# A buffer of zeros moved onto a table's place, with a wait for its transfer

## What is computed

```python
ada = c_act @ w_ada[l] + b_ada[l]
sh_m, sc_m, g_m, sh_f, sc_f, g_f = jnp.split(ada, 6, axis=-1)
h = modulate(rms_norm(x), sh_m, sc_m)          # h*(1+scale)+shift
proj = h @ w_in[l]
z, u = proj[..., :D_SHIFT], proj[..., D_SHIFT:]
...
# s5_mix(u, ...): 32 groups, 16 channels and 64 states each
abar_re = mag * jnp.cos(dt * a_im)             # and abar_im
bbar_re = coef_re[..., None] * b_re - coef_im[..., None] * b_im
bu_re = jnp.einsum("gpc,btgc->tbgp", bbar_re, ug)
_, _, s_re, s_im = lax.associative_scan(_ssm_combine, (a_seq_re, a_seq_im, bu_re, bu_im), axis=0)
y = einsum("gcp,tbgp->btgc", c_re, s_re) - einsum("gcp,tbgp->btgc", c_im, s_im) + d_skip * ug
```

## Time and profile before

| what | us |
|---|---|
| time, median of 3 runs | 1687.66 |
| lowest and highest of them | 1687.02, 1688.44 |
| the profiled execution's own time | 1687.02 |
| its span | 1685.2 |

### The profile page before, as it was taken

One profiled execution on the slowest core, in us unless ns is written; L12 is line 12 of the kernel. 1 busy time (PEld: TensorE's weight loads), 2 busy tenths in 40 slices (PEclk: granted clock), 3 DMA queues, 4 the chain that ended last, 5 costly groups with the idle time before them and its releaser, 6 DMA issues.

```text
span 1685.2 us, 23778 instructions
## 1 busy us (share of the span) xinstructions
PE 1507.8 (89%) x10024; PEld 1173.4 (70%) x10024; DVE 812.8 (48%) x1291; ACT 581.0 (34%) x1002; POOL 267.4 (16%) x224
## 2 busy tenths in 40 slices
PE   6979877877889999999989899998898999998989
PEld 3657666865668888888866687766686667766767
DVE  7783439623653233223354554546534455445552
ACT  4355231125333222222223434224522444232441
POOL 0000323000101011100012223222201233222220
PEclk9999987988999999999979999998998999999999
DMA  9212572162122222233221121111122111111121
GB/s 367 69 59 61 94 140 104 52 226 88 63 75 88 100 94 94 95 125 100 89 88 40 48 76 63 62 39 50 52 99 96 36 63 59 67 65 36 50 88 63
DMA packets 51849, 144.17 MB, mean 86 GB/s; under 512 B 13216, under 2 KB 17952, under 8 KB 50976
## 3 DMA queue, kind: packets, MB, share of 16 engines
q1 hardware_dynamic: 51744, 142.65, 26.4%
HBM read 137.95 MB, written 4.69 MB: 85 GB/s over the span
## 4 chain that ended last, share of the span: by engine, by line
PE 69%; DVE 14%; ACT 9%; issue 4%; POOL 2%; DMA 1%; SPq 0%; DVEq 0%; ACTq 0%
PE b L391 68%; ACT arena L2103 5%; DVE arena L1245 4%; DVE ring L1245 2%; DVE arena L1253 2%; ACT ring L2106 1%; PE b L394 1%; ACT L2103 1%; POOL arena L2734 1%; DVE arena L1933 1%; DVE X L1245 1%; ACT arena L2106 1%; DVE arena L2066 1%; DMA arena<-scr_yd 1%; DVE arena L1891 1%
## 5 line engine op out<-in xcount | busy, mean ns | idle before, releaser
L391 PE MATMUL b<-tile,ring 128*128 128x512 f32 x2288 | 702.9, 402 | 19.8 <-DVE ring L1245 9.2
L391 PE MATMUL b<-HR,ring 128*128 128x512 f32 (+1 forms) x1888 | 626.2, 408 | 63.1 <-DVE ring L1245 35.1
L391 PEld LDWEIGHTS b<-tile,ring 128*128 128x128 f32 x2288 | 437.5, 192 | 127.6 <-issue 19.5
L391 PEld LDWEIGHTS b<-HR,ring 128*128 128x128 f32 (+1 forms) x1888 | 363.6, 193 | 165.2 <-issue 61.0
L1245 DVE TENSOR_TENSOR ring<-ring,ring 128x1024 fp32r<-128x1024 f32 x186 | 256.1, 1379 | 299.9 <-ACT ring L2106 299.0
L391 PE MATMUL b<-arena 64*64 64x64 f32 (+10 forms) x3072 | 237.5, 289 | 42.9 <-issue 24.6
L2106 ACT ACTIVATE ring<-ring 128x1024 fp32r<-128x1024 f32 x186 | 195.7, 1054 | 213.9 <-PE b L391 213.4
L391 PEld LDWEIGHTS b<-arena 64*64 64x64 f32 (+5 forms) x3072 | 153.6, 150 | 115.8 <-issue 80.7
L2106 ACT ACTIVATE arena<-b 128x512 f32<-128x512 f32 (+3 forms) x136 | 74.4, 570 | 254.3 <-PE b L391 206.3
L1245 DVE TENSOR_TENSOR arena<-arena 128x512 f32<-128x512 f32 (+7 forms) x194 | 100.3, 549 | 71.2 <-ACT arena L2103 50.2
L2731 POOL TENSOR_TENSOR tile<-arena,tile 128x512 fp32r<-128x512 f32 x38 | 51.0, 1348 | 462.2 <-ACT tile L2106 462.2
(11 more groups left out here) (112 smaller groups left out, 1018.8 us busy)
## 6 DMA issues: line engine op xcount, KB each, us to landing
ring<-in_ws SPq DMA_DIRECT2D x218, 512.0 KB, 3.5
arena<-in_ws SPq DMA_DIRECT2D x15, 512.0 KB, 15.4
arena<-in_lw SPq DMA_DIRECT2D x2, 1280.0 KB, 5.6
X<-in_xT SPq DMA_DIRECT2D x2, 1024.0 KB, 6.2
arena<-scr_kpad SPq DMA_DIRECT2D x8, 256.0 KB, 12.5
X<-in_xT SPq DMA_DIRECT2D x1, 2048.0 KB, 15.3
outT<-X SPq DMA_DIRECT2D x8, 256.0 KB, 2.0
arena<-in_cst SPq DMA_DIRECT2D x1, 1088.0 KB, 5.0
```

The costliest lines, as they stand in the source:

```text
L391: return self.e.matmul(out, lhsT, rhs, start=start, stop=stop, skip_group_check=True)
```

## The change

The source of the zeros becomes a full 16 x (32 x 112) buffer over the first 14 KB of `VT`, where it was 16 x 112 at a place of its own, read 32 times over by a step of zero. Since `VT` is now written over what the transfer reads, VectorE waits for the transfer's landing before the first write of `VT`.

```diff
@@ Plan.views
-        self.TT, self.VM, self.zero = R(110, 32, 128), R(110, 16, 2, 128), R(131.75, 112)[0:16]
+        self.TT, self.VM, self.zero = R(110, 32, 128), R(110, 16, 2, 128), R(110, 32, 112)[0:16]
@@ Vector.s5_tables
             V(BB[:, ri], BB[:, ri], t, op)
         yield
+        self.wait_ge(k.s("kpad", 16), "zero")
         for dst, n, p0, p1, a, b, op in (
                 (VT[:, :, 0], 8, PR, PI, BB[:, 0], BB[:, 1], ALU.subtract),
@@ Sync.program
         self.wait_ge(k.s("mat_pool"), "zero")
-        self.e.dma_start(d["kpad"].rearrange("g c n -> c g n")[:, :, 0:112],
-                         k.zero.unsqueeze(1).broadcast_to((16, 32, 112))).then_inc(*k.s("kpad", 16).inc("zero"))
+        self.e.dma_start(d["kpad"].rearrange("g c n -> c g n")[:, :, 0:112], k.zero).then_inc(*k.s("kpad", 16).inc("zero"))
```

## The result

The changed kernel took 1712.67 us, the median of 4 runs (1705.23 to 1714.95), beside 1688.05 us for the kernel before in the same comparison (4 runs, 1687.02 to 1697.04). The ratio is 1.0127, with a 95% interval of 1.0081 to 1.0173. On 1688.05 that is 21.4 us, interval 13.7 to 29.2. The prediction was 1708.0, in a range of 1705.5 to 1711.5, slower. By the ratio the time is 1688.05 x 1.0127 = 1709.5; the median as it stands lies 1.2 us over the range's upper end.

A forecast was written before the change was run, and what follows sets the result against it. The start was taken as bound by a chain through ScalarE and VectorE, not TensorE. Stall 21.1 less slack 0.97 gave 20.2, plus 0.3 for the clock: 20.5 us over the 1687.66 median, said as 1708, range 1705.5 to 1711.5.

The forecast's parts named there:

- The landing: Zeros' transfer, last in SyncE's full queue: lands at 39.3 us, 16.1 after issue, as before; floor 38.6, the last unit's landing.
- The early landing: Rival: the 16.1 us are this transfer's own slowness and vanish; landing at 27.8, +8.7 us, 1696.4 us; chance 0.03.
- The stall and the slack: VectorE before the first VT operation: 21.1 us of stall less 0.97 of slack, a shift of 20.2 us.
- The memset: GpSimd's zeroing at the kernel's start: 32 times the columns, about 3.0 us, hidden, cost nothing.
- The late rival: Rival: late landing or late memset, zeros landing at 43.2 or 44.2, +24 to +25 us, 1712 or 1713; chance 0.07.
- The issue: SyncE issuing the zeros: 2.98 us before, perhaps 0.43 without the step of zero; saving hidden, 0.
- Who waits behind it: After VectorE's stall: TensorE, SyncE's later loads and ScalarE resume 20.2 us later; at most about 0.5 us comes back.
- The other side: Rival, not slower: a later stretch paced by the weight stream takes the stall back, 1688 us; chance 0.03.
- The clock after the rest: TensorE's lower-clock stretch after its longer idle time, at the projection's start: costs 0 to 0.6 us more, 0.3 taken.
- Each stretch as long as before: Sign for the changed profile: stretches to the end unchanged; wrong if first projection matmul to end differs by over 1 us.
- with about 1 us of scatter: Allowance for scatter and reshuffling later in the kernel, widening the forecast's 1707.2 to 1709.3 to 1706 to 1710 us.
- The upper bound of 21.6 us: Upper end of the forecast slowdown, whose lower end, 19.5 us, was the landing's floor; this forecast had chance 0.87.

The follow-up runs named there:

- the runs behind 12 to 18 units: Changed kernel with the zeros' transfer issued after 12, 14, 16 or 18 of the 20 weight units; 8.1, 8.8, 17.3 and 14.4 us over the kernel before.
- place of W: Changed kernel with the zeros over table W instead of VT and the wait ahead of W's first write; 1692.55 us, ratio 1.0008 to the kernel before.
- W ahead of VT: Changed kernel with the passes over W before those over VT, wait at VT's first pass; 1691.33 us, ratio 0.9991 to the kernel before.
- wait alone: Kernel before with only the added wait, the zeros' old place and transfer form kept; 1710.01 us, ratio 1.0112 to the kernel before.
- the second comparison: Changed kernel measured once more, unchanged, against the kernel before; 1710.52 us beside 1692.64, ratio 1.0104, 17.6 us slower.

## Why the prediction was right

*The landing.* Right. 16.1 us after the issue, as before, with the last unit's floor beneath it. The early landing, the rival at 1696, is refuted by the profile after and by the runs behind 12 to 18 units. No run came near the 2.5 us estimated for this transfer from the fit in the Trainium skill (DMA: Bandwidth & Descriptors, Anatomy of one DMA). That section gives the fit for transfers issued by GpSimd, while SyncE issues this one. It landed 16.1 us after its issue behind the 20 units and still 9.3 us after it ahead of them all, so the measurement decides.

*The stall and the slack.* Right: 21.09 us of stall and 19.9 of start shift, for 21.1 and 20.2. The queue got to the zeros 0.14 us earlier than in the profile before.

*The memset.* Right: 3.08 us for a predicted 3.0, hidden. The late rival did not occur.

*The issue.* I left open whether the 2.98 us came from the step of zero. They did not: the old and the new source both took 2977 ns behind 20 units, and the new one 334 ns ahead of them all. Its place among the units made the difference, though not evenly: behind 6, 12, 14, 16 and 18 units the issue took 1192, 2888, 1078, 1082 and 1085 ns. Why is open. It cost nothing in any of these, as I said.

*Who waits behind it.* Right: SyncE's next loads came at 48.51 in place of 28.61, and from the first projection matmul to the next cut the changed kernel took 129.78 us for 129.93; no later transfer took the stall back. The other side (not slower) did not occur.

*The clock after the rest.* Mis-sized, by little: 0.3 us taken, 0.0 seen in this pair of profiles, with some 3.1 us at the lower clock after 23.9 us of rest as after 3.95. The other traces show that this stretch varies by itself and does not follow the rest: 4.8 us after 3.95 us (place of W), 5.4 after 3.67 (W ahead of VT), 5.8 after 13.1 (behind 12 units), 5.0 after 24.0 (wait alone).

*"Each stretch as long as before", "with about 1 us of scatter".* This is the term that failed, and I had named it as what would make me wrong: the profiled execution was 5.9 us longer from the first projection matmul to the end. The mechanism of the change is not at fault. The place-of-W execution had no stall and ended 8.3 us late all the same. 21 runs of the kernel before lay 6.9 us apart in one comparison and 8.5 in another. A scatter of some 2 us to either side of a median of few runs should have been in the range; the three runs shown beforehand (1687.02 to 1688.44) were closer together than this kernel's runs usually are. The upper bound of 21.6 us in the forecast has no term behind it: 20.2 and the whole 0.6 of the clock make 20.8.

*How much was luck.* The stall and its shift were forecast well. That the time fell inside a range of 6 us is in part luck: by the ratio of the first comparison it is 1709.5, by that of the second on the same 1688.05 it would be 1705.6, 0.1 us inside the lower end. And the forecast of 20.5 us lies 0.2 over the end of the second comparison's interval (15.1 to 20.3).

*Left open.* Six of seven comparisons gave 1 to 3 us less than their start shift. It may be the chance of each comparison, or a delay of the start may change on average where the clock falls later. The differences of time don't separate the two. The profiled executions show no such gain: behind the first projection matmul those with a stall took 0.7 us more in the mean than those without, with a spread of 8 us in each group.

## What to carry to other kernels

A buffer can be put on another's place for nothing only if the transfer that reads it has landed before the first write. For that, look at the landing and at the queue ahead of the transfer, not at the issue or the size: here 224 KB landed 39 us into the kernel behind twenty units of 512 KB, and 13 us into it ahead of them. Look at the landing in absolute time, since the issue is held up by the same units. If the place has to be shared, move the transfer ahead of the bulk loads, or do first the work that doesn't write there; both brought back what the stall had cost, to within about 2 us in the first case and 3 in the second. And take a kernel's scatter from many runs before giving a range of a few microseconds.

## What the runs showed that I had not expected

- Two executions with the same work and the same start differed by 8.3 us at the end, with the difference growing in steps. About half of it was TensorE's busy time at a lower mean clock; in the last stretch of the changed kernel's, 222 matmuls took 54.66 us at a mean clock of 0.94 for 51.86 at 1.00. Where the low stretches fall in this kernel with its many short waits differs from one execution to the next.
- The time that SyncE spends on issuing one transfer depends on its place in the queue, and not evenly: for the same bytes, 334 ns with five transfers ahead, 2888 ns behind twelve more units, 1078 behind fourteen, 2977 behind twenty.
- The issue itself moves with the load on the queue. Behind 6 to 20 units the zeros landed 14.6 to 16.6 us after their issue, so that this time alone looks like a fixed cost of the transfer; only the run ahead of all units (9.3 us) and the landing in absolute time tell it apart.
